# Expert matmuls in plain fp32 on four column groups of TensorE, instead of three fp32r products of split weights on the whole array

## The reference, cut to what matters

```
def swiglu(h, w1, w3, w2):
    return (jax.nn.silu(h @ w1) * (h @ w3)) @ w2

def moe_ffn(h, router_w, w1, w3, w2):
    logits = (h @ router_w).astype(jnp.float32)
    vals, idx = lax.top_k(logits, TOP_K_EXPERTS)
    ...
    for e in range(N_EXPERTS):
        out = out + gate[..., e:e + 1] * swiglu(h, w1[e], w3[e], w2[e])
    return out
```

## Time and profile before

| what | value |
|---|---|
| median of 3 runs | 1678.23 us (1673.94 to 1680.12) |
| profiled execution: its time | 1676.77 us |
| profiled execution: its span, first to last instruction | 1675.0 us |
| PE busy | 1641.8 us (98%) |
| DVE busy | 1363.3 us (81%) |
| ACT busy | 1064.2 us (64%) |
| mean granted TensorE clock | 0.993 |

### The profile page before, as it was taken

The page is one execution under the profiler, slowest core; times in us unless marked ns, Lnnn a source line. Parts: engine busy times, 40 slices in busy tenths (PEclk is TensorE's granted clock), DMA queues, the critical chain, the costliest instruction groups (busy, mean ns, idle before and its releaser), DMA issues.

```text
span 1675.0 us, 24200 instructions
## 1 busy us (share of the span) xinstructions
PE 1641.8 (98%) x8916; PEld 1384.0 (83%) x8916; DVE 1363.3 (81%) x1134; ACT 1064.2 (64%) x894; POOL 444.8 (27%) x541
## 2 busy tenths in 40 slices
PE   8999999999999999999999999999999999999998
PEld 5887888999888788878888888888888888888886
DVE  5799675556669876688888988888888988888888
ACT  4345456444455544577777777777777777777775
POOL 8966802999152341233000000000000000000200
PEclk9999999999999999999999999999999999999999
DMA  8443556556445355389999999999999999999995
GB/s 294 158 158 115 175 189 217 181 190 219 150 152 176 126 176 185 121 314 396 384 381 388 365 384 385 367 386 385 369 387 382 372 384 377 379 383 370 391 395 195
DMA packets 212459, 481.57 MB, mean 287 GB/s; under 512 B 7936, under 2 KB 32640, under 8 KB 212144
## 3 DMA queue, kind: packets, MB, share of 16 engines
q1 hardware_dynamic: 207456, 463.34, 76.8%
q0 software_dynamic: 4512, 16.78, 2.7%
q10 hardware_dynamic: 432, 0.65, 0.1%
HBM read 473.40 MB, written 7.34 MB: 287 GB/s over the span
## 4 chain that ended last, share of the span: by engine, by line
PE 67%; DVE 2%; ACT 1%; issue 0%; DVEq 0%; ACTq 0%
PE ps L655 20%; PE ps L657 20%; PE ps L656 20%; PE ps L1330 1%; PE ps L701 1%; PE ps L703 1%; PE ps L702 1%; DVE w_lo L286 1%; PE ps L891 0%; PE ps L1406 0%; PE ps L1283 0%; ACT w_hi L280 0%; PE ps L1387 0%; DVE keybias L2171 0%; DVE keybias L2169 0%
## 5 line engine op out<-in xcount | busy, mean ns | idle before, releaser
L286 DVE TENSOR_TENSOR w_lo<-raw,w_hi 128x2048 fp32r<-128x2048 f32 (+1 forms) x433 | 1005.9, 2326 | 220.6 <-ACT w_hi L280 219.1
L280 ACT ACTIVATE w_hi<-raw 128x2048 fp32r<-128x2048 f32 (+1 forms) x433 | 830.0, 1918 | 410.1 <-PE ps L657 323.0
L655 PE MATMUL ps<-w_hi,xg_hi 128*128 128x512 f32 x896 | 354.5, 396 | 1.2 <-DVE w_lo L286 1.2
L657 PE MATMUL ps<-w_hi,xg_lo 128*128 128x512 f32 x896 | 349.5, 390 | 0.0
L656 PE MATMUL ps<-w_lo,xg_hi 128*128 128x512 f32 x896 | 349.0, 390 | 0.0
L655 PE MATMUL ps<-w_hi,hidT_hi 128*128 128x512 f32 x520 | 203.2, 391 | 0.0
L656 PE MATMUL ps<-w_lo,hidT_hi 128*128 128x512 f32 x520 | 202.5, 389 | 0.0
L657 PE MATMUL ps<-w_hi,hidT_lo 128*128 128x512 f32 x520 | 202.4, 389 | 0.0
L657 PEld LDWEIGHTS ps<-w_hi,xg_lo 128*128 128x128 f32 x896 | 168.2, 188 | 35.8
L655 PEld LDWEIGHTS ps<-w_hi,xg_hi 128*128 128x128 f32 x896 | 168.3, 188 | 35.4 <-DVE w_lo L286 1.7
L656 PEld LDWEIGHTS ps<-w_lo,xg_hi 128*128 128x128 f32 x896 | 168.5, 188 | 33.4
(11 more groups left out here) (432 smaller groups left out, 2409.5 us busy)
## 6 DMA issues: line engine op xcount, KB each, us to landing
raw<-moe_w SPq DMA_DIRECT2D x336, 1024.0 KB, 6.2
raw<-w_in SPq DMA_DIRECT2D x44, 1024.0 KB, 5.5
raw<-ffn_w SPq DMA_DIRECT2D x33, 1024.0 KB, 5.4
raw<-w_o SPq DMA_DIRECT2D x8, 1024.0 KB, 5.0
raw<-w_out_a SPq DMA_DIRECT2D x4, 1024.0 KB, 5.3
raw<-w_out_c SPq DMA_DIRECT2D x4, 1024.0 KB, 5.2
raw<-w_out_b SPq DMA_DIRECT2D x4, 1024.0 KB, 5.1
raw<-w_in SPq DMA_DIRECT2D x4, 904.0 KB, 7.4
```

Of the source, the lines that this page charges most:

```text
L280: act.activation(w_hi[:, n % SPLIT, 0:width], raw[:, n % RAW, 0:width], ACT.Copy)\
L286: dve.tensor_tensor(w_lo[:, n % SPLIT, 0:width], raw[:, n % RAW, 0:width], w_hi[:, n % SPLIT, 0:width].bitcast(F32), ALU.subtract)\
L655: pe.matmul(dst, x_hi, hi, start=first, stop=False, skip_group_check=True)
L657: return pe.matmul(dst, x_lo, hi, start=False, stop=last, skip_group_check=True)
```

## The change

- `SLOTS` is 96 in place of 128 (three tiles of 32 slots). Should an expert have more tokens, up to two further rounds would run.
- An expert's K tile is made of plain fp32 matmuls that read `raw` directly, by `four_tiles`: three with 32 slots each as stationary columns 0 to 31, 32 to 63 and 64 to 95 of the array, over the first 384 of the 512 output columns (`WIDE`), and then three on columns 96 to 127, one for each tile of slots, over the last 128. The output of a K tile is so 128 partitions by 384 columns of a bank.
- The experts' chunks are no longer split; SP refills a `raw` buffer when PE has used it (`used`). All elementwise work on the hidden values is 384 wide in place of 512, three transposes take the place of four, and one copy by DVE (`hidden`) that of the high and low parts.
- The result of an expert has to be put back in order: `rows_out` and `y` copy the part of partitions 96 to 127 in three pieces of 32 partitions.
- The router's product is plain fp32 with `y_back` as a buffer for the transposed tokens, and the gather of expert 0 is one fp32 pass over `h_all` in place of two fp32r passes over `h_hi` and `h_lo`.
- The bias and scale of the variance's root move from DVE to ACT.

```
-SLOTS = P
+SLOTS = 96
+ROUNDS = -(-SEQ // SLOTS)
+TILE = 32
+TILES = SLOTS // TILE
...
+WIDE = HALF * TILES // 4
...
-            def load_at(n, turns, src):
+            def load_at(n, turns, src, read=lo_done):
...
-                        load_at(m + half, turns, w[:, bass.ds(row, 4), bass.ds(col, HALF)])
+                        load_at(m + half, turns, w[:, bass.ds(row, 4), bass.ds(col, HALF)], used)
...
-                        pe.matmul(dst, hT_hi[:, k, tok], router_hi[:, k, :], start=b == 0 and k == 0, stop=False,
-                                  skip_group_check=True)
-                        pe.matmul(dst, hT_hi[:, k, tok], router_lo[:, k, :], start=False, stop=False,
-                                  skip_group_check=True)
-                        mm = pe.matmul(dst, hT_lo[:, k, tok], router_hi[:, k, :], start=False, stop=k == KD - 1,
-                                       skip_group_check=True)
+                            pe.wait_ge(S["hT_hi_done"], 12 + 2 * b + k // 4 + 1)
+                        mm = pe.matmul(dst, y_back[:, b, 0, tok], router_sb[:, k, :], start=b == 0 and k == 0,
+                                       stop=k == KD - 1, skip_group_check=True)
...
+                def loaded(m, turns):
+
+                    pe.wait_ge(raw_full[m % RAW], 16 * (m // RAW + 1) + 16 * turns)
+
+                def four_tiles(bank, x_of, w, first, last):
+
+                    for g in range(TILES):
+                        pe.matmul(ps[tile_rows(g), bank, 0:WIDE], x_of(g), w[:, 0:WIDE], start=first, stop=last,
+                                  skip_group_check=True, tile_position=(0, TILE * g))
+                    for g in range(TILES):
+                        mm = pe.matmul(ps[SLOTS:P, bank, g * P:(g + 1) * P], x_of(g), w[:, WIDE:HALF],
+                                       start=first and g == 0, stop=last, skip_group_check=True,
+                                       tile_position=(0, SLOTS))
+                    return mm
...
-                        pe.wait_ge(lo_done, m + 1 + 6 * turns)
+                        loaded(m, turns)
                         for k in range(4):
                             kk = 4 * half + k
-                            mm = three(ps[:, which, :], xg_hi[:, kk, :], xg_lo[:, kk, :], m,
-                                       lambda w: slot_view(w, m, (4, HALF))[:, k, :], kk == 0, kk == KD - 1)
+                            mm = four_tiles(which, lambda g: xgT[:, kk, tile_rows(g)],
+                                            slot_view(raw, m, (4, HALF))[:, k, :], kk == 0, kk == KD - 1)
...
-                    for k in range(4):
+                    for k in range(TILES):
                         tr = pe.transpose(ps[:, 4, k * P:k * P + P], hid[:, k * P:k * P + P], ident[:, :])
...
+                def rows_out(e):
+
+                    act.wait_ge(S["rows_stored"], 16 * e + 16)
+                    rows = y_sb[:, :].rearrange("s (h n) -> s h n", h=2)
+                    act.activation(rows[:, :, 0:WIDE], ps[0:SLOTS, 2:4, 0:WIDE], ACT.Copy).then_inc(S["y_taken"], 1)
+                    for g in range(TILES):
+                        act.activation(rows[tile_rows(g), :, WIDE:HALF], ps[SLOTS:P, 2:4, g * P:(g + 1) * P],
+                                       ACT.Copy).then_inc(S["y_taken"], 1)
...
+                    act.activation(y_hi[:, at:at + WIDE], ps[0:SLOTS, 2 + half, 0:WIDE], ACT.Copy)\
+                       .then_inc(S["y_hi_done"], 1)
+                    for g in range(TILES):
+                        act.activation(y_sb[tile_rows(g), at + WIDE:at + HALF],
+                                       ps[SLOTS:P, 2 + half, g * P:(g + 1) * P], ACT.Copy)\
+                           .then_inc(S["y_moved"], 1)
+                    act.wait_ge(S["y_moved"], moved)
+                    act.activation(y_hi[:, at + WIDE:at + HALF], y_sb[:, at + WIDE:at + HALF], ACT.Copy)\
+                       .then_inc(S["y_hi_done"], 1)
...
-                    lo(n0 + 6, turns)
-                    lo(n0 + 7, turns)
-                    lo(n0 + 8, turns)
-                    hidden_lo(prev, 4)
-                    lo(n0 + 9, turns)
-                    times_up(this, w3_at, turned)
...
+                    hidden(turned)
+                    times_up(this, w3_at, turned, WIDE)
```

More of the change, by code:

```diff
@@ L609, in down @@
                         row = value(sp, K2 * e + 4 * t + 2 * half)
-                        load_at(m + half, turns, w2e[:, bass.ds(row, 2), :])
+                        load_at(m + half, turns, w2e[:, bass.ds(row, 2), :], used)
                 def expert(e, last):
@@ L1333, in down @@
                 def down(n, i, turns, first=False, middle=None):
-                    pe.wait_ge(S["hidT_lo_done"], i)
-                    for half in range(2):
[L1337 to L1345, removed]
+                    pe.wait_ge(S["hidT_copied"], i - DENSE_STRIPES)
@@ new lines, in down @@
+                    for chunk in range(2):
+                        m = n + chunk
+                        loaded(m, turns)
+                        for k in range(2):
+                            for half in range(2):
+                                mm = four_tiles(2 + half, hidden_tile(hidT, 2 * chunk + k),
+                                                slot_view(raw, m, (2, D))[:, k, half * HALF:(half + 1) * HALF],
+                                                first and chunk == 0 and k == 0, False)
+                            if middle is not None and chunk == 0 and k == 0:
+                                middle()
+                        mm.then_inc(used, 1)
@@ L1360, in last_down @@
-                            for k in range(2):
-                                mm = pe.matmul(dst, xg_hi[:, 2 * chunk + k, :], lo[:, k, cols], start=False, stop=False,
-                                               skip_group_check=True)
+                            if half == 0:
+                                loaded(m, turns)
+                            for k in range(2):
+                                mm = four_tiles(2 + half, hidden_tile(last_hidT, 2 * chunk + k),
+                                                slot_view(raw, m, (2, D))[:, k, half * HALF:(half + 1) * HALF],
+                                                False, chunk == 1 and k == 1)
@@ L1515, in _ @@
             with pe.If(most_tokens > SLOTS):
-                experts(1)
+                for rnd in range(1, ROUNDS):
+                    experts(rnd)
         @block.scalar
@@ L1995, in expert @@
-                    if rnd == 0 and not last:
-                        act.wait_ge(S["rows_stored"], 16 * e + 16)
-                        act.activation(y_sb[:, :], banks(2, 2), ACT.Copy).then_inc(S["y_taken"], 1)
-                    for half in range(2 if last or rnd > 0 else 0):
-                        if last and half == 1:
-                            act.wait_ge(used, n0 + 6 + 6 * (turns + t))
-                        act.activation(y_hi[:, half * HALF:(half + 1) * HALF], ps[:, 2 + half, :], ACT.Copy)\
-                           .then_inc(S["y_hi_done"], 1)
@@ L2016, in experts @@
-                split_hi(act, n0 + 3)
+                        xg(e + 1)
+                        up(i, t + 1, turns + t)
+                        act.wait_ge(used, n0 + 10 + 6 * (turns + t))
+                        if rnd == 0:
+                            rows_out(e)
+                        else:
+                            y(e, 0)
+                            y(e, 1)
+                        return
+                    if rnd == 0:
+                        act.wait_ge(S["rows_stored"], 16 * EXPERTS)
@@ L2687, in expert @@
                     stripe(i, t, turns + t - 1)
[L2688 to L2693 removed]
                     if last:
+                        hidden(value(dve, i + t + 1 - DENSE_STRIPES), last_hidT)
                         if rnd == 0:
```

386 lines of the change are left out of this document (145 added, 241 removed).

## The result

The changed kernel takes 1712.25 us (median of 4 runs, 1711.64 to 1713.3), the kernel before 1678.65 in the same comparison: a ratio of 1.0206 (95% interval 1.0185 to 1.0227). It is slower by 2.1%; I had predicted 1662 us and a range up to 1702. The profiled execution took 1713.3 us with a span of 1711.6.

A forecast was written before the change was run, and what follows sets the result against it. The prediction took PE to bound the kernel, with the loads close behind. Its terms, -32.3 - 6.7 + 11.7 - 3.2 - 1.9 + 0.1 + 16.3, gave -16.0 us and 1662 us, range 1643 to 1702.

The forecast's parts named there:

- plain stripe: On PE, a stripe of 24 K tiles, three transposes and two changes of tiling takes 16.3 us, against 16.81 before.
- K tiles: In the experts, the fourth column group sets the pace: 0.656 us against 0.680, 1344 times, -32.3 us.
- transposes: One transpose fewer in each of 56 stripes, 0.12 us each: -6.7 us.
- changes of tiling: PE switching between whole array (transposes) and column groups (K tiles): 126 times 0.093 us, +11.7 us.
- way to the first expert: From first router matmul to first expert matmul: 32 router records in place of 48, -3.2 us.
- first stripe: The first expert stripe no longer waits for splits: -1.9 us.
- end: After the last matmuls: no wait for hidden values, but five copies of y in place of one: +0.1 us in all.
- jump back: End of PE's outer expert loop body: each of six jumps waits for one instruction packet, 2.7 us, +16.3 us.
- 5.4 to 6.3 if a second one is: Upper bound in us for PE's stall at one jump back, if a second instruction packet is waited for.
- Rival 1: At the jumps back, the loop body is kept in the engine, nothing is refetched: 1646 us, chance 0.20.
- Rival 2: A jump back waits for two packets, its target lying near a packet's end: 1684 us, chance 0.12.
- Rivals 3 and 4: Column groups wait at K tile borders, up to +125 us, chance 0.18; records start in program order, +1150, chance 0.02.

The follow-up runs named there:

- light loads: The changed kernel with each load of expert weights cut to an eighth of its columns, all instructions kept, result left wrong: 1687.67 us (one run).
- shifted kernel: The changed kernel with TensorE's code behind the warm-up moved on by 128 instructions, half a packet, through a longer warm-up: 1701.06 us, ratio 1.0123.
- written-out kernel: The changed kernel with TensorE's loop over seven experts written out, inner loops kept, so no jump back at an expert's end: 1648.07 us, ratio 0.9821.
- short: The changed kernel with TensorE's loop body cut from five written stripes to three, some 1800 instructions: 1721.65 us, ratio 1.0263.
- two-jump: The changed kernel with two experts in a body of TensorE's outer loop, two jumps back in place of six: 1669.07 us, ratio 0.9928.

## Why the prediction was wrong

Step by step, what the traces say of the changed kernel:

| step of the prediction | predicted | measured |
|---|---|---|
| a plain stripe (K tiles, transposes, changes of tiling) | 16.3 us | 16.34 |
| from the first transposes to the last-but-one, without the jumps | -26.3 (my terms for 54 of 56 stripes) | -26.0 |
| way to the first expert | -3.2 | -3.4 (12.83 for 16.27) |
| first stripe, to its transposes | -2.4 (1.9 of waits, 0.5 as any stripe) | -2.4 (15.86 for 18.27) |
| start of the router | nothing | -1.4 |
| end, from the last-but-one transposes | -0.4 (+0.1, and 0.5 as any stripe) | -0.4 |
| **jump back, six times** | **+16.3** | **+70.2** |
| instruction packets an expert | some 11 | 13 to 15 |

The changes, without the first and the last row, add up to -16.0 us predicted and +36.6 measured.

**The step that failed is "The jump back", by its size.** The mechanism was right, and where it acts: packets all through the experts, long branches at the end of the outer body, PE idle only there. The price of one was 2.7 us in the forecast and is 11.7. It had four parts, and I had only the first, at the wrong size:

1. *The branch*: 3.59 us taken, 6.20 on average measured. The row was from a place where the DMA engines had nothing to do; with light loads it is 3.8. **+2.6.**
2. *A second packet*: none taken, 4.59 us on average measured (4.03 at the first jump). The shifted kernel makes it 0.27. **+4.6.**
3. *The clock*: none taken. An interval loses 11.7 us and PE is idle for 9.4 of them (56.6 / 6); the other 2.3 go by in matmuls at 1.2 GHz. The shifted kernel loses 7.5 a jump with 5.3 idle and the one with light loads 7.3 with 5.6, so some 2 there too. **+2.3.**
4. *The sequencer's lead*: 0.87 us taken for 16 records, 6.20 + 4.59 - 9.43 = 1.36 measured. In the trace 19 matmul records start after the branch has, and the last one's own length comes on top. **-0.5.**

2.7 + 2.6 + 4.6 + 2.3 - 0.5 = 11.7 us.

Of the bounds, "5.4 to 6.3 if a second one is" was still only half, because both packets were priced by the branch of a quiet moment and nothing was said of the clock. That the clock falls at times was in the rows, have 0.83 over 20 us; I used it for the router alone and did not ask what it does behind an idle stretch.

**Rival 1**, the body is kept, did not come about, but with its jumps written out the kernel takes 1648 us where this rival had 1646. **Rival 2**, two packets, is what happened; its argument, that a target near a packet's end gives too few instructions to cover the next, is shown by the shifted kernel. Its price of 3.6 us for the second packet is near the 3.2 of the kernel that loads little. **Rivals 3 and 4**, column groups that wait for each other, are out: the fourth group's records start 0.1096 us apart, which makes 0.658 us for a K tile, where 0.656 was predicted. A stripe of 16.34 us then leaves 0.55 for its transposes and changes of tiling, as predicted together.

The sequencer's lead explains most of why a jump costs less in the kernel before, 8.2 us in place of 11.7. Its matmul records last 0.23 us and those of the changed kernel 0.055 on average (12 in 0.658 us). When the branch starts, 15 records are still to start there and 19 here, and these cover 3.7 us of the fetch there and 1.4 here. The rest of the difference, 1.2 us, is the fetch, 9.5 and 9.6 us from the branch's start to the first matmul there and 10.8 here. A change to more and shorter instructions makes the body longer and the cover thinner at once.

## What to carry to other kernels

Count the instructions of a loop body before and after a change: a plain fp32 matmul on TensorE is four where an fp32r one is two, and column groups multiply them. When a body of TensorE passes some 1400 instructions, as the trace counts them with weight loads and branches, write the loop out; here that turned a change that lost 2.1% into one that gains 1.8%, with every matmul unchanged. And price a stall by a row that was taken under the same load, and add what the clock does behind it.

## What the runs showed of the hardware

- TensorE keeps a loop body of 1396 instructions and not one of 1661; beyond that the length doesn't matter (1661 and 2283 cost the same). The Trainium skill (Runtime: NRT & Kernel Launch, "Instruction fetch mechanics") gives 2048 instructions as the size of that memory; the bodies of 1661 and 1800 instructions are under it and were fetched anew at each turn, so as a limit for loops the measurement decides. Why it is lower isn't shown.
- In the changed kernel a branch to unfetched code takes 3.8 us in the median with the DMA engines 23% busy and 6.1 with them full, and 3.2 or 4.6 more pass before the first matmul when the target stands badly in its packet (0.3 when it was moved by 128 instructions). In the kernel before, with the DMA engines full, the branch takes 3.6 to 4.3 us and 5.3 to 6.3 more pass.
- Read forwards, code costs next to nothing even with full DMA queues: 122 packets and 1.4 us of waits for instructions in the written-out kernel.
- After 4.9 to 10.0 us without a matmul (all jumps of the changed kernel, of its shifted, light, short and two-jump versions and of the kernel before with two experts in a body) TensorE's granted clock is 0.50 for the first 2.7 to 5.9 us of matmuls.
- Very small fp32 matmuls in a row don't keep the clock up. Records of 8 columns start every 0.11 us at a granted clock of 0.99, as records of 128 columns do; after 3 us of them the clock is 0.50, they start every 0.21 us, and the large matmuls behind them are slow for 6 us. 8 x 126 of them made the kernel before 1878.85 - 1678.15 = 200.7 us longer, this slow stretch behind them included.
